# Expert rows picked by one full-precision product instead of two rounded ones, with their scale moved to Silu and the weights, and an eighth place for expert weights

## The reference

```python
g_prob = softmax(xt @ wg + bg)                  # 8 groups
g_p, g_idx = top_k(g_prob, 1)
e_in = (xt @ we + be) of the chosen group       # 8 experts in it
e_val, e_loc = top_k(e_in, 2)
weight = g_p * softmax(e_val)
def expert_chunk(args):
    xc, e = args
    return (jax.nn.silu(xc @ w_gate[e]) * (xc @ w_up[e])) @ w_down[e]
y = zeros.at[slot_tok].add(ybuf * slot_w[:, None])
```

## Time and profile before

| what | value |
|---|---|
| median of 3 runs | 2002.98 us (2002.28 to 2003.38) |
| span of the profiled execution (first to last instruction) | 2002.0 us |
| time of the profiled execution beside its span | the profile gives none |
| busy: PE | 1888.2 us, 94% of the span |
| busy: DVE | 693.8 us, 35% |
| busy: ACT | 561.2 us, 28% |
| busy: POOL | 287.7 us, 14% |
| mean granted clock of PE | 0.989 |
| moved by DMA | 505.88 MB |

### The profile page before, as it was taken

The page is one execution under the profiler, slowest core; times in us unless marked ns, Lnnn a source line. Parts: engine busy times, 40 slices in busy tenths (PEclk is TensorE's granted clock), DMA queues, the critical chain, the costliest instruction groups (busy, mean ns, idle before and its releaser), DMA issues.

```text
span 2002.0 us, 28095 instructions
## 1 busy us (share of the span) xinstructions
PE 1888.2 (94%) x11846; PEld 1341.4 (67%) x11846; DVE 693.8 (35%) x1639; ACT 561.2 (28%) x1163; POOL 287.7 (14%) x240
## 2 busy tenths in 40 slices
PE   6999999999999998999999999999998999999997
PEld 5887777777777676788875666555555655556554
DVE  4331222543856658711151222213222222222222
ACT  5322232323444444432321221212112121211211
POOL 2433433433000003355200000000000000000000
PEclk9999999999999999999999999999999999999999
DMA  9452322324222213145469999999999999999994
GB/s 288 124 161 75 79 79 69 84 64 95 43 58 59 53 44 126 43 140 187 147 282 415 429 417 427 426 428 428 426 426 427 420 422 420 422 424 410 427 427 184
DMA packets 175661, 505.88 MB, mean 253 GB/s; under 512 B 52642, under 2 KB 135970, under 8 KB 148906
## 3 DMA queue, kind: packets, MB, share of 16 engines
q1 hardware_dynamic: 173226, 495.63, 64.7%
q0 software_dynamic: 2304, 8.39, 1.0%
HBM read 495.85 MB, written 16.53 MB: 256 GB/s over the span
## 4 chain that ended last, share of the span: by engine, by line
PE 91%; issue 3%; DVE 3%; ACT 2%; DMA 1%; POOL 0%; SPq 0%; POOLq 0%; ACTq 0%; DVEq 0%
PE banks L916 25%; PE banks L1310 19%; PE banks L1340 12%; PE banks L1070 9%; PE banks L1283 6%; PE banks L1311 3%; PE banks L1230 3%; PE banks L1022 2%; PE banks L1003 2%; PE banks L1050 2%; PE banks L1231 1%; PE banks L965 1%; PE banks L1150 1%; PE banks L1010 1%; PE banks L1324 0%
## 5 line engine op out<-in xcount | busy, mean ns | idle before, releaser
L916 PE MATMUL banks<-ht_rounded,ring_rounded 128*128 128x512 f32 x1056 | 361.2, 396 | 4.9 <-ACT at_region L1453 4.9
L916 PEld LDWEIGHTS banks<-ht_rounded,ring_rounded 128*128 128x128 f32 x1056 | 196.8, 189 | 58.9 <-issue 14.2
L1311 PE MATMUL banks<-at_region,ht_region 128*64 128x256 f32 x896 | 200.1, 382 | 0.0
L1310 PE MATMUL banks<-at_region,ht_region 128*64 128x256 f32 x864 | 192.9, 382 | 6.0 <-issue 6.0
L804 POOL TENSOR_TENSOR ring_rounded<-ring_region,ring_rounded 128x512 fp32r<-128x512 f32 x100 | 127.2, 1304 | 469.9 <-ACT ring_rounded L1392 469.9
L2126 DVE TENSOR_TENSOR ring_region<-ring_region,banks 64x256 f32<-64x256 f32 x64 | 27.1, 423 | 381.3 <-ACT ring_region L1644 381.2
L1310 PEld LDWEIGHTS banks<-at_region,ht_region 128*64 128x64 f32 x864 | 118.5, 138 | 58.6 <-issue 19.1
L804 POOL TENSOR_TENSOR ring_rounded<-ring_region,at_rounded 128x512 fp32r<-128x512 f32 (+1 forms) x100 | 126.6, 1298 | 203.9 <-ACT at_rounded L1392 203.9
L1644 ACT ACTIVATE ring_region<-banks 64x256 f32<-64x256 f32 x64 | 24.2, 378 | 457.1 <-PE banks L1311 457.1
L916 PE MATMUL banks<-ht_rounded,at_rounded 128*128 128x512 f32 x352 | 143.9, 409 | 5.6 <-ACT at_region L1453 4.9
L1310 PE MATMUL banks<-x_region,ht_region 128*64 128x256 f32 x608 | 136.2, 383 | 2.6 <-issue 2.6
(11 more groups left out here) (290 smaller groups left out, 3390.5 us busy)
## 6 DMA issues: line engine op xcount, KB each, us to landing
at_region<-in_w_gate SPq DMA_DIRECT2D x27, 2048.0 KB, 21.1
at_region<-in_w_up SPq DMA_DIRECT2D x27, 2048.0 KB, 19.9
at_region<-in_w_down SPq DMA_DIRECT2D x27, 2048.0 KB, 23.2
x_region<-in_w_gate SPq DMA_DIRECT2D x19, 2048.0 KB, 21.8
ring_region<-in_w_in SPq DMA_DIRECT2D x36, 1024.0 KB, 6.0
x_region<-in_w_up SPq DMA_DIRECT2D x18, 2048.0 KB, 18.9
x_region<-in_w_down SPq DMA_DIRECT2D x17, 2048.0 KB, 25.2
ring_region<-in_w_down SPq DMA_DIRECT2D x10, 2048.0 KB, 23.2
```

The costliest lines, as they stand in the source:

```text
L916: ins = mm(out, w[:, k, 0:width], h[:, k, :], start=k == 0 and i == 0, stop=k == KT - 1 and i == 2)
L1310: mm(PJ[0:CAP, 0:D_EXPERT], x, gate[j], start=j == 0, stop=j == KT - 1)
L1311: ins = mm(PJ[CAP:2 * CAP, 0:D_EXPERT], x, up[j], start=j == 0, stop=j == KT - 1)
```

## The change

The rows are no longer split in `hi` and `lo`. PE picks from `xg[b]` itself, in plain float32, with one product for each part j; the part is read with a step of 16 floats from the rows as gathered. `pick` is plain float32 too. ACT's `split_high` and DVE's `split_low` are gone.

The factor `row_rstd` is no longer in the picked inputs. It comes in twice behind the gate and up products: Silu gets it as its scale for each slot, and the router's weights are multiplied by the token's `rstd`, which makes up for the up products. The scale of each slot is found by 8 small products per group (`pick` of each expert by `row_rstd`, 64 x 8 each) ahead of the group's first gate product; ACT copies their 64 x 64 to `rstd_of_slot` ahead of the group's first Silu.

The SBUF of `hi` and `lo` becomes an eighth place for weights. SP loads chunk 8 into it ahead of its wait for the first gather. The filler products ahead of the first pick go from 20 to 6.

```diff
-FAST_SLOTS = SLOTS + 1
+FAST_SLOTS = SLOTS + 2
...
         chunk = [region(a, D_EXPERT * KT) for a in (AT0 + 12 * KB, AT0 + 28 * KB, AT0 + 44 * KB, X0, X0 + 16 * KB, RING0,
-                                                            HT0 + 16 * KB)]
+                                                            HT0 + 16 * KB, MIX0 + 16 * KB)]
...
-        hi = region(MIX0 + 16 * KB, KT, P, memory=rounded)
-        lo = region(MIX0 + 24 * KB, KT, P, memory=rounded)
...
-        pick = region(RING0 + 28 * KB, PER * CAP, memory=rounded)
+        pick = region(RING0 + 28 * KB, PER * CAP)
...
+        rstd_of_slot = consts[:, C_BUCKET:C_BUCKET + PER * N_GROUPS]
...
+        RSTD = D_EXPERT + 2 * CAP
...
             sp.wait_ge(row2_sum, NT * NT)
+            load_chunk(SLOTS + len(ONCE) + 1)
             sp.wait_ge(xg_in[0], 16)
...
-            for n in range(SLOTS + len(ONCE) + 1, CHUNKS - 3):
+            for n in range(SLOTS + len(ONCE) + 2, CHUNKS - 3):
...
-            keep_busy(20)
+            keep_busy(6)
...
             def pick_half(g, h):
...
+                pe.wait_ge(xg_in[g % 2], g // 2 * 16 + 16)
                 place, turn = half_places(g, h)
+                rows = xg[g % 2].rearrange("r (p k) -> r k p", k=KT)
                 for j in range(KT):
-                    if j % 4 == 0:
-                        pe.wait_ge(split_a, g * 4 + (j // 4 + 1))
-                        pe.wait_ge(split_v, g * 4 + (j // 4 + 1))
...
-                    mm(place[turn[j]][:, 0:HALF], hi[:, j, :], slots, start=True, stop=False)
-                    mm(place[turn[j]][:, 0:HALF], lo[:, j, :], slots, start=False, stop=True).then_inc(picked, 1)
+                    mm(place[turn[j]][:, 0:HALF], rows[:, j, :], slots, start=True, stop=True).then_inc(picked, 1)
...
                 fence(c, g)
+                if e8 == 0:
+                    for i in range(PER):
+                        mm(PJ[0:CAP, RSTD + i * N_GROUPS:RSTD + (i + 1) * N_GROUPS], pick[:, i * CAP:(i + 1) * CAP], row_rstd,
+                           start=True, stop=True)
                 for j in range(KT):
...
-            def split_high(c, g, i, b, q):
...
-                fn(hi[:, 4 * q:4 * q + 4, :], rows[:, 4 * q:4 * q + 4, :], ACT.Copy,
-                   scale=row_rstd[:, bass.ds(g, 1)]).then_inc(split_a, 1)
...
-                fn(silu[0:CAP, :], PJ[0:CAP, 0:D_EXPERT], ACT.Silu).then_inc(silu_done, 1)
+                if e8 == 0:
+                    fn(rstd_of_slot[0:CAP, :], PJ[0:CAP, RSTD:RSTD + PER * N_GROUPS], ACT.Copy).then_inc(rstd_copied, 1)
+                    act.wait_ge(rstd_copied, c * N_GROUPS + g + 1)
+                fn(silu[0:CAP, :], PJ[0:CAP, 0:D_EXPERT], ACT.Silu,
+                   scale=rstd_of_slot[0:CAP, bass.ds(e8 * N_GROUPS + g, 1)]).then_inc(silu_done, 1)
...
-            def split_low(c, g, i, b, q):
...
-                v.scalar_tensor_tensor(lo[:, 4 * q:4 * q + 4, :], rows[:, 4 * q:4 * q + 4, :], row_rstd[:, bass.ds(g, 1)],
-                                       hi[:, 4 * q:4 * q + 4, :].bitcast(F32), ALU.mult, ALU.subtract).then_inc(split_v, 1)
...
             link(v.reciprocal(wts[:, 0, :], one_e))
+            link(v.tensor_tensor(wts[:, 0, :], wts[:, 0, :], rstd, ALU.mult))
```

More of the change, by code:

```diff
@@ L582, in hybrid_block_moe_kernel @@
         g_copied, xg_in, out_landed = sem("g_copied"), [sem(f"xg_in{b}") for b in range(2)], sem("out_landed")
-        split_a, split_v, own_slots, pick_ready, picked = (sem("split_a"), sem("split_v"), sem("own_slots"),
+        rstd_copied, own_slots, pick_ready, picked = (sem("rstd_copied"), sem("own_slots"),
                                                            sem("pick_ready"), sem("picked"))
@@ L1229, in pick_half, with pick_rows @@
                     slots = pick[:, h * HALF:(h + 1) * HALF]
-                    mm(place[turn[j]][:, 0:HALF], hi[:, j, :], slots, start=True, stop=False)
-                    mm(place[turn[j]][:, 0:HALF], lo[:, j, :], slots, start=False, stop=True).then_inc(picked, 1)
-            def pick_rows(c, g, first):
+                    mm(place[turn[j]][:, 0:HALF], rows[:, j, :], slots, start=True, stop=True).then_inc(picked, 1)
+            def pick_rows(c, g, i, b, first):
                 done = c * N_GROUPS + g
@@ L1239, in pick_rows @@
                     pe.wait_ge(idx_ready, c + 1)
-                pe.wait_ge(split_a, done * 4 + 4)
-                pe.wait_ge(split_v, done * 4 + 4)
+                pe.wait_ge(xg_in[b], (c * (N_GROUPS // 2) + i) * 16 + 16)
+                rows = xg[b].rearrange("r (p k) -> r k p", k=KT)
                 for j in range(KT):
@@ L1245, in pick_rows @@
                         pe.wait_ge(y_v, c * E_ALL + g * PER)
-                    i = last_user(TURN4, j)
-                    if i is not None:
-                        pe.wait_ge(xT_v if i % 2 else xT_a, copies_ahead(c, g) + (i // 2 + 1))
+                    at = last_user(TURN4, j)
+                    if at is not None:
+                        pe.wait_ge(xT_v if at % 2 else xT_a, copies_ahead(c, g) + (at // 2 + 1))
                     fence(c, g)
-                    mm(place[TURN4[j]], hi[:, j, :], pick, start=True, stop=False)
-                    mm(place[TURN4[j]], lo[:, j, :], pick, start=False, stop=True).then_inc(picked, 1)
+                    mm(place[TURN4[j]], rows[:, j, :], pick, start=True, stop=True).then_inc(picked, 1)
             def chunk_landed(c, g, e8, kind):
@@ L1345, in expert, with group @@
                 ins.then_inc(down_done, 1)
-            def group(c, g, begins, final):
+            def group(c, g, i, b, begins, final):
                 for e8 in range(PER):
@@ L1354, in group @@
                 else:
-                    pick_rows(c, g + 1, False)
+                    pick_rows(c, g + 1, i + b, 1 - b, False)
             pick_half(0, 0)
             for g in range(N_GROUPS):
-                group(0, g, g == 0, g == N_GROUPS - 1)
+                group(0, g, g // 2, g % 2, g == 0, g == N_GROUPS - 1)
             pe.wait_ge(most_ready, 1)
@@ L1366, in _ @@
                     place_marks(c)
[L1367 to L1371, removed]
+                    pick_rows(c, 0, 0, 0, True)
+                    group(c, 0, 0, 0, True, False)
+                    group(c, 1, 0, 1, False, False)
+                    with pe.Fori(1, N_GROUPS // 2 - 1) as i:
+                        for b in range(2):
+                            group(c, i * 2 + b, i, b, False, False)
+                    group(c, N_GROUPS - 2, N_GROUPS // 2 - 1, 0, False, False)
+                    group(c, N_GROUPS - 1, N_GROUPS // 2 - 1, 1, False, True)
             with pe.Else():
@@ L1608, in _ @@
             fn(g_tmp[:, 1], g_tmp[:, 0], ACT.Exp).then_inc(g_exped, 1)
-            def split_high(c, g, i, b, q):
-                if q == 0:
-                    act.wait_ge(xg_in[b], (c * (N_GROUPS // 2) + i) * 16 + 16)
-                rows = xg[b].rearrange("r (p k) -> r k p", k=KT)
-                fn(hi[:, 4 * q:4 * q + 4, :], rows[:, 4 * q:4 * q + 4, :], ACT.Copy,
-                   scale=row_rstd[:, bass.ds(g, 1)]).then_inc(split_a, 1)
             def copy_picked(c, g, first):
@@ L1657, in group @@
                         square_rows(c, g - 1, 1 - b)
-                    if not final and e8 in (5, 6):
-                        for q in range(2 * e8 - 10, 2 * e8 - 8):
-                            split_high(c, g + 1, i + b, 1 - b, q)
                 if final:
@@ L1666, in group @@
                     copy_picked(c, g + 1, False)
-            act.wait_ge(idx_ready, 1)
-            for q in range(4):
-                split_high(0, 0, 0, 0, q)
             act.wait_ge(e_diff, 1)
@@ L1679, in _ @@
                 with act.Fori(1, PASSES + 1) as c:
-                    act.wait_ge(idx_ready, c + 1)
-                    for q in range(4):
-                        split_high(c, 0, 0, 0, q)
                     copy_picked(c, 0, True)
@@ L2055, in _ @@
             build_pick(0, 0)
-            for q in range(4):
-                split_low(0, 0, 0, 0, q)
             def copy_picked(c, g, first):
@@ L2155, in group @@
                         build_pick(c, g + 1)
-                    if not final and e8 in (5, 6):
-                        for q in range(2 * e8 - 10, 2 * e8 - 8):
-                            split_low(c, g + 1, i + b, 1 - b, q)
                 if fast(c) and not final:
@@ L2188, in _ @@
                     build_pick(c, 0)
-                    for q in range(4):
-                        split_low(c, 0, 0, 0, q)
                     copy_picked(c, 0, True)
```

## The result

The changed kernel takes 2015.34 us (median of 4 runs, 2014.77 to 2015.75) against 2003.18 us of the kernel before (4 runs): a ratio of 1.0057, 95% interval 1.0042 to 1.0071. It is slower by 0.6%, and the interval leaves no doubt of the sign. The forecast was 2006.8 us; the time lies 8.5 us above it and 1.3 us above the top of the range (2014).

A forecast was written before the change was run, and what follows sets the result against it. The prediction took PE to bound the changed kernel: span 2002.0, less 25.3 us in hand, plus 29.1 of added PE work, is 2005.8; with 1.0 from span to median, 2006.8 us. Range: 1997.5 to 2014.

The forecast's parts named there:

- PE has 25.3 us in hand: Expert stage: waits and slow slices, 23.5 + 1.8 us, that PE can fill before its own work sets the end.
- PE sets the pace afterwards, without waits and slow slices: Changed expert stage: no idling ahead of gate products, no granted 0.50 after 1100, DMA share now and then below 1.0.
- loads of 128 columns follow each other by 0.11 us (20 in 2.1 us), so they hide behind 0.216: Picks: weight loads stay hidden behind full-precision product instructions, so a new pick takes 32 x 0.216 = 6.90 us.
- strided loads: Rival, picks: loads with a step of 16 floats outlast products; at four times today's load 113 us, 2120; 3%.
- first halves +2.03: First pick of each group: 6.90 us instead of 4.87, +2.03 each, 14.2 us for seven.
- Second halves +1.14: Second pick of each group: 6.90 us instead of 5.86, last product ending 0.1 later; 9.1 us for eight.
- Scale products 0.9: Eight small products ahead of each group's first gate product, on PE's path: 0.9 us a group, 7.2 in all.
- Net 1.4 us earlier at the start: First group: without the split its pick starts 2.95 us earlier but takes 6.90 instead of 5.34, net 1.4 earlier.
- All transfers run 4.9 us ahead: Weight transfers: the eighth place with chunk 8 loaded early puts them 4.9 us ahead of today, up to 7.
- the transfers keep the pace: Rival, expert stage: the last wait for weights still decides and comes 4.9 to 7 us earlier; 1999.2, down to 1997; 16%.
- The sum: Whole kernel: 29.1 us added to PE less 25.3 in hand, taking the span from 2002.0 to 2005.8.
- the 1.0: Whole time: the median of the runs was taken to lie 1.0 us above the profile's span.

The follow-up runs named there:

- packed_in_before: The kernel before, with ACT alone writing the scaled rows packed in full precision and one full product for each part: 2010.37 us, ratio 1.0030.
- pick_step1: The changed kernel, with each pick product reading 128 neighbouring floats of the gathered rows instead of every 16th: 2010.39 us, ratio 1.0037.
- no_scale: The changed kernel without the eight scale products of a group and the copy of their result; Silu reads constants: 2008.89 us, ratio 1.0026.
- seven_places: The changed kernel with seven places for weights again, chunk 8 waiting for the place of chunk 0: 2018.59 us, ratio 1.0069.
- rounded_step16: The kernel before, with its high and low parts in the order of the rows, so loaded with a step of 16 floats: 2012.94 us, ratio 1.0047.

## Why the prediction was wrong, step by step

- *PE has 25.3 us in hand* was right. Added up over the periods between gate products, what lies above the undisturbed period of each kind comes to 25.4, and `packed_in_before` used it up.
- *PE sets the pace afterwards, without waits and slow slices* was right, in each point: no idle line, no granted 0.50 from 1100 on until PE's work ends, a DMA share below 1.0 in places.
- *"loads of 128 columns follow each other by 0.11 us (20 in 2.1 us), so they hide behind 0.216"* failed. It is the step at which the size went wrong. With a step of 16 floats the loads of a product take 0.12 us longer (307 ns against 188), so they follow each other at 0.22 or more and pace the product stream; in second halves a product that takes up a used bank starts 0.26 to 0.28 behind the last one, five times a pick, where `pick_step1` has 0.22 throughout. The edit `pick_step1` alone measures this: 7.5 us of stage, in one trace each. The prediction had this as its rival "strided loads", with the right place and with the right point from which it decides (twice today's load), at 3% and, for four times, 113 us. It set the chance low because of the transposes of x2, which load with the same step in 196 ns. That row was from another kind of instruction, and the kernel before has no product whose loaded operand has that step.
- The Trainium skill, SBUF — State Buffer, section "Door 1: The DMA port swizzle", says that a 16-byte line needs two hits or more for full bandwidth, and that each access which crosses to a new line pays. The loads of products at steps 1, 2, 4 and 16 (190, 196, 329 and 307 ns) fit the two hits; the transposes at step 16 (196 ns) do not. The section also gives 4 fp32 as how far one can stride for free; read as a step, the 329 ns of step 4 speak against it. The Trainium skill, TensorE: Matmul & The Clock Gate, section "LDWEIGHTS (loading the stationary operand)", gives the time of a load by its columns, and for 128 its formula comes to 107 ns, an estimate. That fits the pace of the packed loads (0.11 us) and not that of the stepped ones (0.22 us).
- By the periods of gate products: *first halves +2.03*: +2.10 with packed loads (`pick_step1`), +2.46 as changed. *Second halves +1.14*: +1.24 and +1.81. With packed loads the copies of the banks held nothing up. *Scale products 0.9*: 0.95, on the path.
- *Net 1.4 us earlier at the start* came out as 0.9 without the scale products (`no_scale`): the pick itself started on time, 8.31 us behind the row indices (11.33 before), but took 7.46 instead of 6.90. With the scale products the first gate product is where it was (16.72 against 16.67).
- *All transfers run 4.9 us ahead* failed, harmlessly. By the landings chunk 9 comes 4.8 us earlier, chunk 40 1.3, and the later ones up to 2.6 later (the last expert's 6 and more), since places come free at PE's pace. `seven_places` shows that nothing hangs on it. With this the rival "the transfers keep the pace" had the wrong price too: it counted on the lead staying to the end.
- The sum: the stage was to grow by 3.8 us and grew by 12.87. Of the 9.1 between, 7.5 is the step. The remaining 1.6 is in packed picks and scale products a little dearer than forecast: 7 x 0.07 + 8 x 0.10 + 8 x 0.05 = 1.7. Outside the stage two more differences nearly cancel: the row indices came 1.6 us earlier in the changed kernel's trace (the two traces of the kernel before differ by 4.2 there), and the run's time lies 2.1 us above its span, not 1.0; the 1.0 compared a profiled span with a median of other runs. 9.1 - 1.6 + 1.1 is the miss of 8.5, within rounding. So even without the step the change would have lost: with it gone the stage is still 5.4 us longer than before.

## What to carry to other kernels

Ask of every operand's view how it lies in memory, not only how many instructions read it: a copy that splits may also pack, and what it packs is paid for again when it goes. Count what the bounding engine has in hand before an edit adds to it; 25 us sounded like room, and the full products alone filled it. And take a row as evidence for an operation only if it is of the same kind of instruction: the transposes' load time misled here about the products'.

## What was new about the hardware

- Transposes load with a step of 16 floats at 196 ns, products at 307 to 316, in full precision and rounded, in the same traces. Why transposes don't pay was not tried.
- A pick paced by its loads loses hardly anything at 1.2 GHz. In `rounded_step16` the granted clock is 0.50 for 3.4 us inside three of the eight first-half picks, and those take 7.37 us against 7.29 of the four between them. In one, from 1269.8 on, behind 1.9 us of picking, PE still has 16 products in 3.40 us, 0.21 each:

```profile
1269.80:1273.20 3.40, 3.40 (x16) 3.40 (x16) 1.89 (x4) 1.63 (x4) 0.00 (x0) 0.50 0.97 414
```
